# The last step of each layer laid out anew, and half of the last coefficient loads issued from ScalarE's queue

## What is computed

```python
for i in range(DEPTH):                 # 2
    norm, mixer, w_out = layers[i]
    x = x + mixer(rms_norm(x, norm)) @ w_out
return rms_norm(x, final_norm)
```

```python
o, _ = banded_attention(q, k, v, SWA_WINDOW - 1, sinks)           # layer 0
return o.reshape(B, S, MIX_WIDTH) * jax.nn.silu(gate)

w = jax.nn.softmax(jnp.stack(lses, axis=0), axis=0)               # layer 1
o = jnp.sum(w[..., None] * jnp.stack(outs, axis=0), axis=0)
return o.reshape(B, S, MIX_WIDTH) * jax.nn.silu(gate)
```

## Time and profile before

| what | value |
|---|---|
| median of 3 runs | 1429.42 us (1428.33 to 1431.09) |
| the profiled execution, its own time | 1429.45 us |
| its span, first to last instruction | 1427.7 us |
| PE busy | 1317.5 us (92% of the span) |
| DVE, ACT, POOL busy | 732.4, 635.2, 394.3 us |
| DMA engines busy | 22.5% (one queue, SP's) |
| mean granted TensorE clock | 0.963 |

### The profile page before, as it was taken

How to read it: one execution, slowest core, us unless ns; L and a number is a source line. 1 busy time by engine, 2 the same in 40 slices (tenths; PEclk the granted TensorE clock), 3 DMA queues, 4 the chain that set the end, 5 groups by cost and what they waited for, 6 DMA issues and landing times.

```text
span 1427.7 us, 24896 instructions
## 1 busy us (share of the span) xinstructions
PE 1317.5 (92%) x8938; PEld 1228.0 (86%) x8938; DVE 732.4 (51%) x2225; ACT 635.2 (44%) x1767; POOL 394.3 (28%) x443
## 2 busy tenths in 40 slices
PE   5899999999399997999999999899999999994996
PEld 5898998987399897999979999899999799983996
DVE  5545453544732524555436764356654367646625
ACT  6344453636511434544436554346444365545011
POOL 2211051330501111131212823106722128223210
PEclk9999999999799998999999999999999999995998
DMA  5011021121435211011021311212310212134522
GB/s 191 17 30 45 23 61 66 45 82 42 159 102 186 76 36 46 15 36 28 18 79 47 87 57 32 59 34 75 93 29 17 80 47 76 54 91 104 148 89 118
DMA packets 101080, 97.32 MB, mean 68 GB/s; under 512 B 30688, under 2 KB 87520, under 8 KB 100960
## 3 DMA queue, kind: packets, MB, share of 16 engines
q1 hardware_dynamic: 100960, 95.73, 22.5%
HBM read 79.46 MB, written 16.25 MB: 67 GB/s over the span
## 4 chain that ended last, share of the span: by engine, by line
PE 84%; DVE 6%; DMA 4%; ACT 2%; POOL 2%; issue 2%; SPq 1%; DVEq 0%; POOLq 0%; ACTq 0%
PE j_bank L1096 58%; PE s_bank L1199 8%; PE o_bank L1232 7%; PE t_bank L1211 6%; PE j_bank L1178 3%; DVE ht_lo L1690 1%; DMA qk<-mix_dram 1%; DVE ht_lo L1568 1%; DMA w_raw<-in_w_out 1%; DMA gate<-in_positions 1%; PE s_bank L1096 1%; PE o_bank L1096 1%; ACT ht_hi L1380 1%; DVE w_lo L1499 1%; SPq L800 1%
## 5 line engine op out<-in xcount | busy, mean ns | idle before, releaser
L1096 PE MATMUL j_bank<-w_hi,ht_hi 128*128 128x384 f32 (+1 forms) x1328 | 454.1, 342 | 15.5 <-DVE ht_lo L1568 7.1
L1096 PE MATMUL j_bank<-w_lo,ht_hi 128*128 128x384 f32 (+1 forms) x1328 | 441.8, 333 | 0.0
L1096 PE MATMUL j_bank<-w_hi,ht_lo 128*128 128x384 f32 (+1 forms) x1328 | 441.4, 332 | 0.0
L970 POOL TENSOR_TENSOR w_lo<-w_raw,w_hi 128x768 fp32r<-128x768 f32 (+1 forms) x60 | 101.0, 1683 | 695.8 <-ACT w_hi L1307 694.7
L1096 PEld LDWEIGHTS j_bank<-w_hi,ht_hi 128*128 128x128 f32 x1328 | 254.6, 192 | 27.8 <-issue 20.3
L1096 PEld LDWEIGHTS j_bank<-w_lo,ht_hi 128*128 128x128 f32 x1328 | 255.0, 192 | 0.0
L1096 PEld LDWEIGHTS j_bank<-w_hi,ht_lo 128*128 128x128 f32 x1328 | 254.2, 191 | 0.0
L1316 ACT ACTIVATE probs<-probs,stat 128x256 f32<-128x256 f32 (+1 forms) x512 | 230.6, 453 | 31.1 <-DVE stat L1531 29.5
L1526 DVE CUSTOM_DVE_ANT_0 probs<-s_bank,masks 128x128 f32<-128x128 f32 (+1 forms) x448 | 142.4, 354 | 135.2 <-PE t_bank L1211 131.5
L722 ACT COPY probs_t<-t_bank 128x256 f32<-128x256 f32 (+1 forms) x128 | 57.9, 452 | 311.4 <-PE o_bank L1232 306.2
L1199 PE MATMUL s_bank<-ks,qs 128*128 128x256 f32 (+1 forms) x1024 | 144.1, 284 | 4.6 <-DVE ks L1585 4.3
(11 more groups left out here) (159 smaller groups left out, 1645.1 us busy)
## 6 DMA issues: line engine op xcount, KB each, us to landing
w_raw<-in_w_qkv SPq DMA_DIRECT2D x64, 384.0 KB, 3.3
coef<-coef_dram SPq DMA_DIRECT2D x96, 128.0 KB, 2.9
w_raw<-in_w_gate SPq DMA_DIRECT2D x32, 256.0 KB, 3.3
mix_dram<-xr SPq DMA_DIRECT2D x12, 512.0 KB, 3.9
w_raw<-in_w_out SPq DMA_DIRECT2D x16, 384.0 KB, 3.5
qk<-mix_dram SPq DMA_DIRECT2D x12, 512.0 KB, 5.1
xr<-in_x SPq DMA_DIRECT2D x8, 512.0 KB, 7.5
out<-xr SPq DMA_DIRECT2D x8, 512.0 KB, 2.7
```

What stands on the lines that cost most here:

```text
L970: pool.tensor_tensor(quarter(n, q, 1), raw_quarter(n, q), quarter(n, q, 0).bitcast(F32), ALU.subtract).then_inc(w_lo_done["p"], 1)
L1096: last = pe.matmul(to, a(x_, kt), b(y_, kt), start=(start and kt == kts[0] and x_ == y_), stop=(stop and kt == kts[-1] and x_ == 1))
```

## The change

It has four parts. In the last step of a layer the gate pieces stand at slots 0, 4, 8, 12, and the coefficients of the last group's first half are turned and copied two slots later (13 for 11). The six tiles are split behind the last step, and their last three loads are issued there too; the output product's first part runs tile by tile over seven rows (`early_rows`) instead of row by row over six tiles. `end_coefs` of the second half is halved: SP issues the loads of head j = 0, ScalarE those of j = 1, behind its six splits. In pair 12 of steps 6, 9 and 12 the first gate piece is put ahead of the fill. GpSimd's `end_mix` waits for the Silu only at the product that reads it.

```diff
@@ -73,7 +73,7 @@
-            _slots.append((JOBS[-1], [0, 2, 4, 6] if _s.last else [12, 13, 14, 15]))
+            _slots.append((JOBS[-1], [0, 4, 8, 12] if _s.last else [12, 13, 14, 15]))
@@ -84,7 +84,7 @@
-            _at += [(3, _now[0] + 1, (0,)), (5, _now[0] + 1, (1,)), (8, _now[0] + 1, (2, 3))]
+            _at += [(3, _now[0] + 1, (0,)), (5, _now[0] + 1, (1,)), (14, _now[0] + 1, (2, 3))]
@@ -136,10 +136,10 @@
-SPLIT_MIX = [8, 9, 10, 11, 14, 15]
-END_FIRST, END_EXP, END_LAST, END_TURN, END_COPY = 8, 9, 10, 11, 11
+EARLY_ORDER = [0, 1, 2, 3, 6, 4, 5]
+END_FIRST, END_EXP, END_LAST, END_TURN, END_COPY = 8, 9, 10, 13, 13
@@ -307,7 +307,7 @@
-    if a == 0 and not by_class(s):
+    if (a == 0 and not by_class(s)) or (a == 12 and not s.last and by_class(STEPS[s.t + 1])):
         work, pieces = pieces[:1], pieces[1:]
@@ -788,16 +797,13 @@
-            def end_coefs(s, r):
+            def end_coefs(s, r, heads):
...
-                    for j in range(2):
...
+                    for j in heads:
+                        sp.dma_start(end_to(s, r, p, j), end_from(s, r, p, j)).then_inc(end_in[3 * r + p], 16)
@@ -906,16 +912,15 @@
-                            for k in range(3, MIX_LOADS):
-                                if slot == max(SPLIT_MIX[k - 3] + 1, 12 if k > 3 else 0):
-                                    mix_load(layer, k)
...
                 last = steps[-1]
+                for k in range(3, MIX_LOADS):
+                    mix_load(layer, k)
                 coef_store(last, 1)
-                end_coefs(last, 1)
+                end_coefs(last, 1, (0,))
@@ -1133,27 +1138,25 @@
+            def early_rows(layer, kt):
...
+                if kt % 4 == 0:
+                    weights_half(job, kt // 4)
+                pe.wait_ge(mix_lo, layer * MIX_TILES + kt + 1)
+                pe.wait_ge(mix_hi, layer * MIX_TILES + kt + 1)
+                for k in EARLY_ORDER:
...
+                    a, b, _ = operands(job, k)
+                    products(out_bank(layer, k), a, b, [kt], kt == 0, False)
@@ -1278,9 +1281,9 @@
-                for k in range(EARLY):
-                    early_row(layer, k)
-                    if k == 1:
+                for kt in range(MIX_LOADS):
+                    early_rows(layer, kt)
+                    if kt == 0:
                         coef_turn(last, 1)
@@ -1378,6 +1381,13 @@
+            def end_coefs(s):
+
+                act.wait_ge(coef_out, 16 * (calls_before(s.t) + 2))
+                act.wait_ge(scored, UNITS * (s.t + 1))
+                for p in range(1 if s.layer == 0 else 3):
+                    act.dma_start(end_to(s, 1, p, 1), end_from(s, 1, p, 1)).then_inc(end_in[3 + p], 16)
@@ -1465,7 +1467,15 @@
-                den_exp(last, 1)
+                act.wait_ge(piece_full, PIECE.filled(last_piece(JOB[("gate", layer, GROUPS - 1)])))
+                for k in range(MIX_LOADS):
+                    act.wait_ge(mix_back[k % 3], 16 * (layer * 2 + k // 3 + 1))
+                    mix_split(layer, k, mix_in[k % 3])
+                    if k == 0:
+                        den_exp(last, 1)
+                    if k == 1:
+                        silu(last)
+                end_coefs(last)
@@ -1854,16 +1864,17 @@
                 coefs_first(last, 1)
+                mix_split(layer, 0, mix_in[0])
+                store_ot(last, 1, 1)
                 coefs_last(last, 1)
-                store_ot(last, 1, 1)
-                coef_copy(last, 1)
+                for k in range(1, MIX_LOADS):
+                    mix_split(layer, k, mix_in[k % 3])
+                    if k == 2:
+                        coef_copy(last, 1)
```

More of the change, by code:

```diff
@@ L664, in splits_of, with coef_from, end_from, end_to @@
             return [(n + 1, 2), (n + 1, 3)] if phase == "next" else [(n + 2, 0), (n + 2, 1)]
+        def coef_from(s, r, p, j):
+            q = 1 if s.layer == 0 else 3
+            return coef_dram[groups_before(s.t), 0:q * NB * R, :].rearrange("(r q n j) i -> r q j n i", r=2, q=q, j=2)[r, p, j]
+        def end_from(s, r, p, j):
+            return coef_from(s, r, p, j).rearrange("(o n) i -> o n i", o=1).broadcast_to([HD, NB, P])
+        def end_to(s, r, p, j):
+            return coef_end[r][p][64 * j:64 * j + 64, :].rearrange("p (n i) -> p n i", n=NB)
         def guard_qkv(eng, key):
@@ L1134, in out_bank @@
                 return bank_[:, 0:out_width(0)]
[L1136 removed]
+            def early_rows(layer, kt):
                 job = ("out", layer, 0)
                 last_step = LAYER_STEPS[layer][-1]
[L1140 to L1156 removed]
+                if kt % 4 == 0:
[3 more added lines that the diff above has]
+                for k in EARLY_ORDER:
+                    if kt == 0 and k not in SPARE:
+                        free_bank(PIECE, piece_empty, job + (k,))
+                    elif kt == 0 and k < 4:
+                        pe.wait_ge(biased, UNITS * (last_step.t + 1))
+                    elif kt == 0 and k < 6:
+                        pe.wait_ge(ot_stored, 4 * (last_step.t + 1))
+                    elif kt == 0:
+                        wait_turn_emptied(pe, (last_step.t, UNITS - 1))
+                    a, b, _ = operands(job, k)
+                    products(out_bank(layer, k), a, b, [kt], kt == 0, False)
             def later_row(layer, r, k):
@@ L1451, in _ @@
                             w_hi(SPLIT_BEHIND.get(s.t, []))
-                        if s.last and SPLIT_MIX[0] - 1 in pair:
-                            silu(s)
-                            act.wait_ge(piece_full, PIECE.filled(last_piece(JOB[("gate", layer, GROUPS - 1)])))
                         for slot in pair:
-                            if s.last and slot in SPLIT_MIX:
-                                k = SPLIT_MIX.index(slot)
-                                act.wait_ge(mix_back[k % 3], 16 * (layer * 2 + k // 3 + 1))
-                                mix_split(layer, k, mix_in[k % 3])
                             if slot == (1 if layer == 0 else 3) and before is not None and before.ends_group:
```

27 lines of the change are left out of this document (2 added, 25 removed).

## The result

The changed kernel takes 1393.01 us (median of 1389.88, 1389.99 and 1396.04; a fourth run, of 4480.9 us, is left out as disturbed), against 1429.28 before: a ratio of 0.9738, 95% interval 0.9705 to 0.977. So it is 36 us faster, where I had forecast 53. Its profiled execution, at 1389.88 us, is 39.6 us under that of before.

A forecast was written before the change was run, and what follows sets the result against it. TensorE's work plus its waits was taken as the bound. Gains of 23.0 (layer 0), 16.2 (layer 1) and 15.0 (steps 6, 9, 12) sum to 54.2 us off 1429.45: 1375.3, given as 1376, range 1369 to 1388.

The forecast's parts named there:

- Steps 6, 9, 12: Pair 12 of these steps: the gate piece fills the 3.6 us rotation wait and the clock recovers; gain 15.0 us.
- The pairs of layer 0: Layer 0's last step: pairs without a piece lose only about 2.0 us, at pair 4; pair 14 begins at 360.5.
- The remark that the third piece covers the Silu: Last step: the third gate piece covers the Silu of the group before, with its table loads.
- The 3.0 us for a pair without a piece: Layer 0's last step: TensorE's own 3.0 us cover VectorE's 1.9 and ScalarE's 2.6, so pairs 10 and 14 cost nothing.
- The drain: Layer 0, pair 14 to the output product: a chain of 11.3 us against 6.1 of TensorE work, 5.2 lost.
- Tile by tile: Output product: 3.6 us of TensorE work a tile exceeds ScalarE's 2.04 and VectorE's 2.9, so no wait between tiles.
- Layer 1: Last layer's end: tile 7 decides, starting at 1334 and not 1350.2 behind GpSimd's 28.3 us chain; gain 16.2 us.
- The clock behind tile 7: After layer 1's wait of 3 to 5 us before tile 7, a lowered clock may cost 1 us.
- ScalarE's loads: Last coefficients' loads halved between SP and ScalarE: ScalarE's half neither gains nor loses.
- the last chain is longer: Rival: GpSimd held up or ScalarE's loads late, so layer 1 gains 6 to 11; 1381 to 1388 us, chance 0.17.
- the pairs lose more: Rival: the clock falls inside the last steps without pieces, a loss of 10 us; 1386 us, chance 0.10.
- The "slower" case: Rival: waits between tiles keep the first product range at 1.2 GHz, 50 us in both layers; 1434 us, chance 0.03.

The follow-up runs named there:

- e1: The changed kernel with the fill put back ahead of the first gate piece in pair 12 of steps 6, 9, 12: 1407.42 us, ratio 0.9832.
- e3: The changed kernel with the last group's gate pieces in pairs 0, 2, 4, 12 in place of 0, 4, 8, 12: 1387.48 us, ratio 0.9696.
- v8: The changed kernel with gate pieces in pairs 0, 2, 4, 12 and layer 0's Silu of the group before moved to pair 12: 1392.94 us, one run.
- e10: The changed kernel run and profiled again with no edit: median 1395.34 us, ratio 0.9736; its profile is of 1396.09 us.
- e6: The changed kernel with the output product again piece by piece over six tiles, the last coefficients turned ahead of it: 1418.51 us, one run.
- e8: The changed kernel with VectorE's subtractions of layer 1's tiles 1 to 5 cut to 16 of 1024 columns: 1386.72 us, one run.
- e5: The changed kernel with the first coefficients' turn ahead of pair 12's gate piece, not behind it: 1387.81 us, ratio 0.9705.
- e2: The changed kernel with SyncE issuing all six loads of the last coefficients and ScalarE none: 1392.53 us, ratio 0.9728.

## Why the prediction was wrong, step by step

The forecast was 1376 (1369 to 1388); the median is 1393, and of the nine runs behind the two medians none is under 1388.9. By the profiled executions the sum of 54.2 misses by 14.6, and by the medians by 18.

- **Steps 6, 9, 12: right.** 15.0 forecast, 14.5 measured, shown by e1 (14.4) as well. The wait and the clock both came back.
- **The pairs of layer 0: the step that failed.** "The exception is pair 4, behind pair 2, whose fill goes ahead of the exponentials" took about 2.0 us for ScalarE's order, and missed that pair 4's scores read what the fill makes. The wait is 2.8 us, and with the clock behind it the place costs 4.6 (e3). Pair 14 started 50.0 us behind the step's start and not 45.9: 2.6 of it at pair 4, 0.6 in pair 12, the rest in pairs 6 to 10. The remark that the third piece covers the Silu was right. The 3.0 us for a pair without a piece was not quite: with fill and Silu covered, v8 takes 46.3 us to pair 14, where four pairs with pieces and three of 3.0 make 43.9. Its three pairs without a piece take 3.53, 3.44 and 3.80.
- **The drain: mis-sized by 1.2.** 11.3 forecast, 12.5 measured (364.20 to 376.71): 0.5 more until the last exponential ends (369.42), 0.5 more for the subtraction (2.86 for 2.4), the rest small gaps between the links. The one wait of 3 to 4 us is there: 3.88.
- **Tile by tile: right in layer 0** (no wait behind tile 0; that B is as before to 0.15 is in part luck, since it was 4.6 more in e10), and all but right in layer 1 (0.35 before tile 1). e6 gives its worth.
- **Layer 1: mechanism right, two terms too small.** Tile 7 decides, with a wait of 5.05 us (3 to 6 forecast), but 89.1 us behind the step's start and not 82.4. The turn was 3.8 us late, again by pair 4 (2.5 of it). GpSimd's chain was 30.9 us and not 28.3; I had named up to 3 us for VectorE's subtractions and put nothing in the sum. e8 shows that it is these. e5 shows that I had the chain's head wrong: not the turn alone, but GpSimd's own weight subtraction holds the first product back, at nearly the same time (in the changed kernel the product waits for its coefficients 0.44 us behind that subtraction). The gain was 9.5 and not 16.2.
- **The clock behind tile 7: 2.4 and not 1.** From tile 7 to the last matmul it was 65.4 us and is 67.8 (66.6 in e10, so this term too differs from one execution to the next). Before, the 6.8 us from tile 7 on ran at 1.00; now at 0.60:

```profile
1308.23:1315.00 6.77, 6.77 (x25) 6.77 (x26) 4.17 (x8) 0.00 (x0) 1.08 (x1) 0.60 0.69 228
```

- **ScalarE's loads: right.** Nothing gained, nothing lost (e2).
- **Added up.** Layer 0 up to the product 5.3, layer 1 up to tile 7 6.7, the clock behind tile 7 2.4, steps 6, 9 and 12 0.5, which less 0.3 elsewhere is the 14.6. The missed reader at pair 4 has 5.1 of it, GpSimd beside VectorE 2.7.
- **The rivals and the range.** Two came partly true together, "the last chain is longer" and "the pairs lose more", at 0.17 and 0.10, and each priced as if it came alone: 1381 to 1388, and 1386. They are not independent: pair 4 delays layer 0's product and layer 1's last chain alike (2.6 and 2.5 us over what I had), so a case with both belonged in the range. The "slower" case has a slip in its sum: 50 us and 1 us before each of six tiles in two layers lead from 1375.3 to 1437, not 1434. And the range took the clock of the one profiled execution of before as certain; e10 shows 6 us between two of one program.

The Trainium skill ("SBUF — State Buffer", two separate sides) says that VectorE and GpSimd hold their shared port one at a time and for a whole instruction. The trace agrees in kind: beside GpSimd's weight subtraction a two-input operation of 128x16 on VectorE took 1.45 us (at 1269.82 in the changed kernel), and the next of its kind, behind it, 0.18. By it I had put layer 1's gain at 9, and 9.5 was measured; but only 2.7 of the missing 6.7 are GpSimd's chain, so that number was right for the wrong reason. Five subtractions all but taken away gave back 4.0 us (e8), where five whole lengths of 1.2 would be 6.

## What to carry to other kernels

When a filler is moved out of a stretch, list everything that it covered, and for each of them the first reader: here a piece had covered both a fill that the next scores read and a Silu on ScalarE, and moving it paid for one with the other. Price what two engines on a shared path do to each other by the rows in which both are at work, and look at what stands ahead on the queue of the engine whose start you count on. Profile one program twice before you read a stretch of 2 us as the work of an edit.

## What the hardware showed that was not expected

The clock does not answer to a wait alone. Behind the same waits of 3.12 to 3.15 and 1.88 us at the end of layer 0's product, the matmuls went on at full clock in one execution of the changed kernel and at 0.57 and 0.55 in the other, and 2.9 of the 4.6 us that B differs by lie behind the first of them. The Trainium skill ("TensorE: Matmul & The Clock Gate", what's actually happening) says that the activity which decides is judged on a rhythm of its own that doesn't start with the kernel, and that cold stretches vary from run to run; the two profiles of the changed kernel agree.

Nor is every slow stretch the clock's. In the changed kernel's pair 12 eight scores take 1.63 us (1.1 to 1.2 elsewhere) and eight turns 1.36 (1.03), with no wait of over 0.3 us ahead of them, and the granted clock of the stretch is 1.00:

```profile
355.03:357.80 2.77, 2.49 (x18) 1.90 (x18) 2.45 (x10) 2.06 (x9) 0.00 (x0) 1.00 0.67 147
```

The same scores take 1.63 us in e10 and e1 too. What slows them no run shows.
